# Query absorption and the first sample scores moved into the cached keys' expansion

## The reference, cut to what matters

```python
# streams: 512 cached latents each, 16 new tokens, 16 heads
kvb    = (c_kv @ w_kv_b).reshape(b, S, 16, 64 + 64)
k_nope = rmsnorm(kvb[..., :64], k_norm)      # needs 1/rms per key and head
v      = kvb[..., 64:]
s = (einsum('bqhd,bkhd->bhqk', q_nope, k_nope)
     + einsum('bqhr,bkr->bhqk', q_rope, k_rope)) * ATTN_SCALE
p = softmax(where(mask, s, -inf)); o = einsum('bhqk,bkhd->bqhd', p, v)
cq = rmsnorm(u @ w_dq, q_norm)               # q_norm: 512 factors
```

## Time and profile before

| | us |
|---|---|
| three runs | 1844.54, 1846.04, 1845.98; median 1845.98 |
| the profiled execution: its own time | 1845.79 |
| its span | 1844.0 |
| PE busy | 1814.8 (98%) |
| DVE busy | 1135.7 (62%) |
| ACT busy | 827.9 (45%) |
| expansion, y = 0 to 7 | about 1281 to 1394 in the span |
| absorption, first scores and units 0 to 15 | about 1395 to 1483 |

### The profile page before, as it was taken

One profiled execution on the slowest core, in us unless ns is written; L12 is line 12 of the kernel. 1 busy time (PEld: TensorE's weight loads), 2 busy tenths in 40 slices (PEclk: granted clock), 3 DMA queues, 4 the chain that ended last, 5 costly groups with the idle time before them and its releaser, 6 DMA issues.

```text
span 1844.0 us, 28274 instructions
## 1 busy us (share of the span) xinstructions
PE 1814.8 (98%) x10567; PEld 1739.3 (94%) x10567; DVE 1135.7 (62%) x1706; ACT 827.9 (45%) x1420; POOL 228.2 (12%) x278
## 2 busy tenths in 40 slices
PE   9999999999999999999999999999998999999998
PEld 9999999799888999999999999996777999999998
DVE  6454447879889745544775454456778856454445
ACT  5333335665564433333563333246665544333333
POOL 1000010311311000011400001122112131000110
PEclk9999999999999999999999999999999999999999
DMA  6434444456352544344343434451124534443442
GB/s 211 134 117 135 137 137 150 154 206 233 122 205 86 192 125 127 123 149 135 117 139 121 134 117 138 137 172 40 47 77 141 173 115 131 129 125 125 148 131 76
DMA packets 68388, 249.49 MB, mean 135 GB/s; under 512 B 8200, under 2 KB 10504, under 8 KB 67024
## 3 DMA queue, kind: packets, MB, share of 16 engines
q1 hardware_dynamic: 58880, 206.86, 36.6%
q0 software_dynamic: 9424, 41.48, 6.6%
HBM read 235.52 MB, written 12.12 MB: 134 GB/s over the span
## 4 chain that ended last, share of the span: by engine, by line
PE 88%; DVE 6%; ACT 3%; issue 1%; DMA 1%; POOL 0%; DVEq 0%; ACTq 0%; POOLq 0%
PE pair L1910 25%; PE pair L1912 25%; PE pair L1911 25%; PE pair L2419 2%; PE pair L2328 2%; PE pair L2330 2%; PE pair L2329 2%; DVE wlo L1242 1%; PE pair L2118 1%; PE pair L2276 0%; PE pair L2448 0%; PE pair L2135 0%; PE pair L1917 0%; PE pair L1919 0%; PE pair L1918 0%
## 5 line engine op out<-in xcount | busy, mean ns | idle before, releaser
L1910 PE MATMUL pair<-xh,whi 128*128 128x384 f32 x1960 | 660.8, 337 | 3.1 <-DVE xl L1252 2.3
L1912 PE MATMUL pair<-xh,wlo 128*128 128x384 f32 x1960 | 655.5, 334 | 0.0
L1911 PE MATMUL pair<-xl,whi 128*128 128x384 f32 x1960 | 655.4, 334 | 0.0
L1242 DVE TENSOR_TENSOR wlo<-raw,whi 128x1024 fp32r<-128x1024 f32 (+3 forms) x371 | 463.9, 1252 | 164.4 <-ACT whi L705 163.6
L705 ACT ACTIVATE whi<-raw 128x1024 fp32r<-128x1024 f32 (+2 forms) x369 | 378.3, 1029 | 266.0 <-PE pair L1912 261.7
L1910 PEld LDWEIGHTS pair<-xh,whi 128*128 128x128 f32 x1960 | 368.1, 188 | 9.9 <-issue 4.1
L1911 PEld LDWEIGHTS pair<-xl,whi 128*128 128x128 f32 x1960 | 368.1, 188 | 1.6 <-issue 1.0
L1912 PEld LDWEIGHTS pair<-xh,wlo 128*128 128x128 f32 x1960 | 368.1, 188 | 0.0
L1262 DVE TENSOR_TENSOR tg<-pair,rstd 128x384 f32<-128x384 f32 x88 | 49.0, 557 | 326.1 <-PE pair L1912 325.4
L1910 PE MATMUL pair<-ah,whi 128*128 128x384 f32 x704 | 238.0, 338 | 0.0
L1912 PE MATMUL pair<-ah,wlo 128*128 128x384 f32 x704 | 237.9, 338 | 0.0
(11 more groups left out here) (406 smaller groups left out, 2199.9 us busy)
## 6 DMA issues: line engine op xcount, KB each, us to landing
raw<-in_stream SPq DMA_DIRECT2D x372, 512.0 KB, 3.6
S<-in_ssm POOLq DMA_DIRECT2D x4, 2048.0 KB, 9.2
out_ssm_s<-S POOLq DMA_DIRECT2D x4, 2048.0 KB, 7.8
seg<-acs_rows POOLq DMA_DIRECT2D x12, 512.0 KB, 5.7
cTb<-in_cacheT POOLq DMA_DIRECT2D x10, 512.0 KB, 4.3
kn<-rs_rows SPq DMA_DIRECT2D x16, 264.0 KB
lowC<-in_cache SPq DMA_DIRECT2D x8, 512.0 KB, 3.2
lowA<-in_cacheT POOLq DMA_DIRECT2D x6, 512.0 KB, 5.3
```

What stands on the lines that cost most here:

```text
L1242: V.tensor_tensor(wlo[:, r, 0:w], raw[:, r, 0:w], whi[:, r, 0:w].bitcast(F32), ALU.subtract).then_inc(lo_ready, 1)
L1910: M(out, whi[:, r, ws], mh_(k), start=first and k == k0, stop=False)
L1911: M(out, whi[:, r, ws], ml_(k), start=False, stop=False)
L1912: ins = M(out, wlo[:, r, ws], mh_(k), start=False, stop=last and k == k1 - 1)
```

## The change

- `absorb(y-1)` is issued after the second item of y = 1 to 7, and `absorb(7)` after the third item of y = 7, with its ACT and DVE halves in the same places. The banks are now 3, 7, 3, 7, 3, 7, 3, 5. POOL loads the four quarters of `wkT` as the prompt's heads are done with that memory.
- In y = 7: `rope_split(0)`, both `keys_split` and `rope_split(1)`, `s_scores(0)`, `s_max(0)`, `s_exp(0)` and the normalisation of unit 0. Streams 0 and 1 get memory of their own for this (`early`), and the last stream's squares go to another place (`sqB`), so that SP may load the factors earlier.
- The factors are made in two halves of four streams. Streams 4 to 7 have their square root in unit 0 on ACT, followed by a reload of the exponential table, their reciprocals in unit 1 on DVE, and the transpose in unit 2 on PE.
- The 512 factors of the query norm move from `gains` to `gq`, at the end of the memory, with a DMA of their own at the start. Two unused columns of `gains` go.

```diff
@@ PE
+            def absorb(j):
+                pe.wait_ge(wkT_ld, 16 * (j // 2 + 1))
+                if j < MH // 2 - 1:
+                    pe.wait_ge(ol_ready, j + 1)
+                else:
+                    pe.wait_ge(p_masked, MH)
...
             for y in range(MH // 2):
+                last = y == MH // 2 - 1
...
                 for i in range(4):
                     past_expand(8 * y + i)
+                    if y and i == 1:
+                        absorb(y - 1)
+                    if last and i == 2:
+                        absorb(y)
+                if last:
+                    pe.wait_ge(past_rstd, 2)
+                    rs_turn(bank[4], 0, 4)
...
-                if y == MH // 2 - 1:
-                    pe.wait_ge(past_rstd, 3)
-                    rs_turn(bank[2], 0, 6)
+                if last:
+                    pe.wait_ge(qc_ev, 8)
+                    pe.wait_ge(rs_ev, 2)
+                    pe.wait_ge(stack_lo, 2)
+                    pe.wait_ge(filled, 5)
+                    s_scores(0)
                 past_expand(8 * y + 6)
                 past_expand(8 * y + 7)
...
-            for j in range(4):
-                absorb(j)
-            absorb(4)
-            absorb(5)
...
-            s_scores(0)
-            absorb(6)
-            absorb(7)
             for u in range(UNITS):
-                if u == 0:
-                    pe.wait_ge(qc_ev, 8)
                 if u + 1 < UNITS:
                     s_scores(u + 1)
-                if u == 1:
-                    pe.wait_ge(past_rstd, 4)
-                    rs_turn(bank[1], 6, 8)
+                if u == 0:
+                    pe.wait_ge(ol_ready, MH // 2)
+                    pe.wait_ge(past_sq, 8 * STREAMS)
                 if u == 3:
                     pe.wait_ge(rs_ev, 3)
                 if u >= 2:
                     s_values(u - 2)
+                if u == 2:
+                    pe.wait_ge(past_rstd, 4)
+                    rs_turn(bank[1], 4, 8)
@@ ACT
                 for i in range(3):
                     past_square(8 * y + i)
+                    if y and i == 1:
+                        absorb_hi(y - 1)
+                if last:
+                    absorb_hi(y)
+                    keys_split(0)
+                    act.wait_ge(rs_turn_ps, 2)
+                    A(rsT[0:4 * MH, :], bank[4][0:4 * MH, 0:3 * P], ACT.Copy)
+                    A(rsT2[0:4 * MH, 0:P], bank[4][0:4 * MH, 3 * P:4 * P], ACT.Copy).then_inc(rs_ev, 1)
                 p_turned(2 * y)
                 p_turned(2 * y + 1)
...
                 past_square(8 * y + 3)
-                if y + 1 < MH // 2:
+                if last:
+                    keys_split(1)
+                    rope_split(1)
+                else:
                     p_exp(2 * y + 2)
...
+                if last:
+                    act.preload_act_table(ACT.Exp)
                 past_square(8 * y + 6)
+                if last:
+                    s_exp(0)
+                if y == MH // 2 - 2:
+                    rope_split(0)
...
+                if u == 0:
+                    A(ksq[:, :, 4:8], ksq[:, :, 4:8], ACT.Sqrt, bias=EPS, scale=1.0 / NOPE).then_inc(past_std, 1)
+                    act.preload_act_table(ACT.Exp)
@@ DVE
                 for i in range(8):
+                    if not more and i == 7:
+                        s_norm(0)
                     past_sums(8 * y + i)
+                    if y and i == 1:
+                        absorbed(y - 1)
...
+                    if not more:
+                        if i == 0:
+                            rope_split(0)
+                        if i in (1, 2):
+                            if i == 2:
+                                absorbed(y)
+                            dve.wait_ge(past_std, 1)
+                            V.reciprocal(ksq[:, :, 2 * i - 2:2 * i], ksq[:, :, 2 * i - 2:2 * i]).then_inc(past_rstd, 1)
+                        if i == 2:
+                            keys_split(0)
+                        if i == 3:
+                            keys_split(1)
+                            rope_split(1)
+                        if i == 5:
+                            s_max(0)
...
+                if u == 1:
                     dve.wait_ge(past_std, 2)
-                    V.reciprocal(ksq[:, :, 6:8], ksq[:, :, 6:8]).then_inc(past_rstd, 1)
+                    for b in (4, 6):
+                        V.reciprocal(ksq[:, :, b:b + 2], ksq[:, :, b:b + 2]).then_inc(past_rstd, 1)
@@ SP and POOL
-            sp.wait_ge(past_sum, 8 * STREAMS)
+            sp.wait_ge(past_sum, 8 * (STREAMS - 1))
             rstd_rows(0)
...
-            for x in range(0, MH, MH // 4):
-                pool.wait_ge(qk_ps, x + MH // 4)
-                pool.dma_start(wkT[0:QD, x:x + MH // 4], T["wkT"][:, x:x + MH // 4]).then_inc(wkT_ld, 16)
+                if b % 2:
+                    x = MH // 4 * (b // 2)
+                    pool.wait_ge(qk_ps, x + MH // 4)
+                    pool.dma_start(wkT[0:QD, x:x + MH // 4], T["wkT"][:, x:x + MH // 4]).then_inc(wkT_ld, 16)
...
+            past_rope(0)
             past_keys(0)
-            past_rope(0)
+            past_rope(1)
+            past_keys(1)
             pool.wait_ge(rs_ev, 2)
```

More of the change, by code:

```diff
@@ L176, in build @@
             lowA = sb("lowA", [P, 4096], F32, mla)
-            lowB = sb("lowB", [P, 4096], F32, mla)
+            with ExitStack() as split:
+                lowB = sb("lowB", [P, 4096], F32, split)
+            early = sb("early", [P, 4096], F32R, mla)
             lowC = sb("lowC", [P, 2048], F32, mla)
@@ new lines, in s_max @@
+            def s_max(u):
+                s, o = u % 2, 64 + 8 * (u % 2)
+                p, r = (t[:, s, 0:KEYS].rearrange("p (a t) -> p a t", a=2) for t in (Pb, kn))
+                dve.wait_ge(pt_ps, MH + max(u - 1, 0))
+                dve.wait_ge(rk_ld[s], 16 * (u // 2 + 1))
+                dve.wait_ge(sc_ps, u + 1)
+                step(V.tensor_tensor(p, pair[1][:, :, 0:KEYS // 2], r, ALU.mult))
+                V.tensor_tensor(p, p, pair[2][:, :, 0:KEYS // 2], ALU.add).then_inc(s_added, 1)
+                dve.wait_ge(s_added, u + 1)
+                step(V.reduce_max(sm[:, o:o + 1], Pb[:, s, 0:KEYS], axis=AX.X))
+                V.tensor_scalar(sm[:, o + 2:o + 3], sm[:, o:o + 1], -SCALE, None, ALU.mult).then_inc(s_max_ready, 1)
@@ L1794, in _, with s_norm @@
+            def s_norm(u):
+                s, o = u % 2, 64 + 8 * (u % 2)
+                dve.wait_ge(s_exp_ready, u + 1)
+                step(V.reciprocal(sm[:, o + 5:o + 6], sm[:, o + 4:o + 5]))
+                V.tensor_scalar(Pb[:, s, 0:KEYS], Pb[:, s, 0:KEYS], sm[:, o + 5:o + 6], None, ALU.mult).then_inc(p_ready, 1)
             past_split(1)
@@ L2331, in past_expand, with s_scores @@
                 ins.then_inc(past_ps, 1)
+            def absorb(j):
+                pe.wait_ge(wkT_ld, 16 * (j // 2 + 1))
+                if j < MH // 2 - 1:
+                    pe.wait_ge(ol_ready, j + 1)
+                else:
+                    pe.wait_ge(p_masked, MH)
+                for k in range(2):
+                    for hh in range(2):
+                        x = 2 * j + hh
+                        ins = M(bank[QC_BANK[j]][:, tiles(2 * k + hh)], wkT[0:QD, x, tiles(k)], Qs[0:QD, :, x, :],
+                                start=True, stop=True)
+                ins.then_inc(qc_ps, 1)
+            def s_scores(u):
+                b, g = divmod(u, 2)
+                if g == 0:
+                    pe.wait_ge(past_lo, STREAMS + b + 1)
+                    pe.wait_ge(stack_lo, 2 + b + 1)
+                if u:
+                    pe.wait_ge(s_added, u)
+                for a in range(2):
+                    t, out = slice(264 * a, 264 * a + 264), pair[1][:, a, 0:264]
+                    for k in range(2):
+                        qh, ql = (q[:, k, b, 8 * g:8 * g + 8, :].rearrange("p h q -> p (h q)") for q in (QCh, QCl))
+                        M(out, qh, keys_hi(b)[:, k, t], start=k == 0, stop=False)
+                        M(out, qh, keys_lo(b)[:, k, t], start=False, stop=False)
+                        M(out, ql, keys_hi(b)[:, k, t], start=False, stop=k == 1)
+                for a in range(2):
+                    ins = M(pair[2][:, a, 0:264], q_stack(b)[0:3 * ROPE, g, :], k_stack(b)[:, 264 * a:264 * a + 264],
+                            start=True, stop=True)
+                ins.then_inc(sc_ps, 1)
             pe.wait_ge(q_kept, 12)
```

218 lines of the change are left out of this document (77 added, 141 removed).

## The result

The kernel after took 1848.99 us (1847.15 to 1850.89, 22 runs), the kernel before 1845.97 (1844.22 to 1847.79, 22 runs): ratio 1.0018, 95% interval 1.0012 to 1.0025. So it is slower by 3.0 us, a little within the 0.2% that the prediction called no change, and 2.0 us over its 1847.0. It looks like a small miss of a small effect. It is not: four terms of about 0.5 to 7 us add up to it, and the prediction had only the smallest at a price of its own. The profiled execution took 1850.78 us, its span 1849.0.

The account below looks back on a forecast made before the run. PE was taken as the bound, busy 1814.8 of 1844.0 us, with 6.25 us of seam waits to win. These go and some 7.5 come; with issue gaps +1.2 on 1845.8 gives 1847.0 us, range 1841.3 to 1850.0.

Parts of the forecast that it names:

- The absorptions lengthen the expansion by 5.6 us: Six absorptions move ahead of item 56, where PE is the bound: expansion 5.6 us longer, what follows shorter by the same.
- The four `wkT` loads are issued a y or more ahead of use ... cost 0, at worst one late quarter, a landing of 4.5 us: Loads on POOL during the expansion: costed at 0, at worst 4.5 us for one quarter landing late.
- The query norm's factors and the 64 bytes less of `gains` cost nothing that a row shows: Load at the start, hidden by 200 us of the first SwiGLU: cost nothing, or 2 us if not hidden.
- The last y and the factors: Layout of y = 7 from item 56: SP may load factors at 12.95 us, landing taken as 3.6, `s_max(0)` at 16.55.
- PE's wait for the turn: In y = 7 PE stands 1.3 us before turning the factors, waiting for DVE's two reciprocals.
- The layout's total: Absorptions 5.6 plus 41.2 us from item 56 to `s_values(2)`: 46.8 against 45.9 before; with issue gaps +1.2 us.
- From there PE is the bound in both kernels: From `s_values(2)`, 41.2 us after item 56, PE is busy 10.00 of 10.00 us, so no further difference.
- The table loads: Two ACT loads around unit 0's square root, 1.28 us each by the row; the skill's page would add 2.8 us.
- (a): Rival: the seam closes as ACT and DVE get through y = 7 faster; 1841.3 us, 1839.5 at most; chance 0.21.
- (b): Rival: seam partly closed, factors land early and ACT's unit 0 queue overlaps better; 2 us won, 1845; chance 0.20.
- (c): Rival: ACT's unit 0 queue longer, each table load holding twice its row; `s_values(0)` 2.6 us later, 1849.6; chance 0.10.
- (d): Rival: the factors land at the upper bound of 6.8 us, +3.2 us, 1850.2; chance 0.05.

Follow-up runs that it names:

- e1: Kernel before with only the query norm's factors moved to `gq` and `gains` 64 bytes per partition smaller: 1839.90 us, ratio 0.9967.
- e3: Kernel after with the second quarter of `wkT` issued before POOL waits to copy the stack: 1842.30 us, ratio 0.9981 to the kernel before.
- e4: e3 with SP's factor loads issued ahead of its value loads: 1840.35 us, ratio 0.9970 to the kernel before.
- e5: e4 with a second pair of ACT table loads in unit 0: 1843.29 us, ratio 0.9983 to the kernel before.
- e6: e4 with the square root and its table loads, the reciprocals and the turn two units later: 1842.33 us, ratio 0.9980 to the kernel before.
- e8: Kernel before's work with small tiles moved so that `ah` and `al` start at 64 modulo 256 bytes: 1839.53 us.
- e11: Kernel before's work with `gains` and `rows` moved to the end, so that `ah` and `al` start at 128 modulo 256 bytes: 1840.06 us.

## Why the prediction was right, and where it was wrong

The forecast of +1.2 us, no change, came near +3.0 by luck: mistakes of +8.7 and -6.1 us cancelled for the most part. The medians divide it so: address -6.1 (e1 less before), `wkT` +6.7 (after less e3), SP's order +2.0 (e3 less e4), the moved work +0.45 (e4 less e1); together +3.0.

**The absorptions lengthen the expansion by 5.6 us: right.** From the first prompt scores to item 56 are 105.8 us before, 110.8 in e4: +5.0, 0.83 for each of six, near the 0.93 of the earlier trace rows. Their halves on ACT and DVE cost nothing, as predicted: PE stays at 13.00 of 13.00 us from 1360.

**"The four `wkT` loads are issued a y or more ahead of use ... cost 0, at worst one late quarter, a landing of 4.5 us": wrong, +6.7.** This is the step that failed. The issue stands a y ahead in the code, but its queue doesn't: POOL waited 15.11 us for ACT to finish the stack, copied four times (2.3 us), and issued the quarter at 1322.96, 0.65 us before PE stood. The landing was 4.5 as the bad end had it, but the sum took 0. The prediction said that POOL "waits for the ends of the y there anyway" and didn't look at the copies between, though the diff has them; and even the bad end left out the lower clock behind the wait, 2.4 us.

**"The query norm's factors and the 64 bytes less of `gains` cost nothing that a row shows": wrong, -6.1.** No row of before could show it, yet its bound was given on one side only (2 us of loss), and no end was set to what a shift of all later tiles may do. The 2.7 ns that it was, over 2112 matmuls, are the second largest term.

**The last y and the factors: right.** In us from item 56:

| | predicted | after | e4 |
|---|---|---|---|
| PE's wait for the turn | 1.3 | 1.00 | 1.00 |
| SP issues the factors | 12.95 | 12.77 | 12.77 |
| `s_max(0)` starts | 16.55 | 17.06 | 16.99 |
| `s_scores(1)` starts | 18.5 | 18.56 | 18.49 |
| `s_values(0)` starts | 30.9 | 31.98 | 31.03 |
| `s_values(2)` starts | 41.2 | 43.06 | 41.93 |

The factors landed in 4.21 us, between the bounds 2.2 and 6.8, 0.6 later than the value taken. (The prediction's own terms for SP, 10.1 + 0.3 + 0.5 + 2.2, make 13.1 and not 12.95, and ACT's from 24.5 make 30.7 and not 30.85. Neither changes the total by more than 0.2.) Wait by wait it was rougher. e4, with the prediction's value in brackets: transposes of unit 0 0.74 (0.3), `s_scores(2)` 1.10 (1.6), transposes of unit 1 0.55 (0.75), `s_scores(3)` 1.56 (0.85), `s_values(0)` 1.18 (2.35), `s_values(1)` 0.93 (0.5). What `s_scores(3)` stood longer is the late load of unit 2's factors, which the prediction left out, and with PE that much later the wait for ACT is shorter. The layout's total in e4 is 5.0 + 41.93 = 46.9 against 45.9 before: +1.0 for a forecast of +1.2. In the kernel after it is 1.1 more, with a clock of 0.66 from 1410 to 1415 and a wait of 1.97 instead of 1.10 before `s_scores(2)`.

**"From there PE is the bound in both kernels": wrong in the kernel after, +2.0.** PE had 8.36 of 10.00 us from 1430. The prediction followed SP's queue only as far as the first factors; before, the same order of SP did no harm: it issued the factors of unit 6 at 1424.69, and DVE used them at 1431.66 without a wait. In the kernel after they went out at 1428.87, and DVE stood 2.46 us for them until 1437.36, PE 1.64 and 0.48. e4, where it is mended, has the 10.00.

**The table loads: right, by the row.** Each took 1.28 us with nothing beside it. The Trainium skill (ScalarE: Activation LUTs, "What ACT_TABLE_LOAD costs") adds about 1380 ns of drain to each load, by which the estimate was 1849.8 us. That is close to what was measured, which shows how little one total proves: e5 has twice the loads and is 2.5 to 2.9 us slower, near the two rows' 2.56 and not the 5.3 of that section, and its queue has no gap.

**The rivals.** (a) and (b), the seam closing: excluded, 7.1 us of waits in e4. (c), ACT's queue longer: the wait exists, but at its row's price. (d), the factors at their bound: 4.21, no; it was the third load of factors that landed late, beside the loads of values that (d) names. What made the time was none of the rivals: an address, a late quarter and SP's order.

## What to carry to other kernels

A load that is written early isn't issued early: walk its queue up to the issue and ask what each instruction ahead of it waits for, for every load of the moved step and once more for the queue at the place where time was won. Removing or adding a small tile moves everything behind it; here that alone was worth 6 us, so time such an edit by itself before reading anything into the rest. When a large reordering comes out near zero, split it before believing that it did nothing: here 6 us of gain hid 9 us of loss. When work moved off a late queue wins nothing, as in e6, follow the chain that ended last to where it is paid again.

## What the runs showed of the hardware

- Where a matmul's moving operand starts in a partition mattered: `ah` and `al` at 0 modulo 256 bytes gave 175.1 ns a matmul of 384 columns, at 64, 128 or 192 it was 172.4 to 172.8. Matmuls of the same shape on `xh` and `xl`, which didn't move, kept their rate (521 in 90 us before and after). Whether it is this operand or another tile moved with it isn't settled.
- A wait of 3.86 us on PE was followed by 4.9 us of matmuls at half the rate, 0.43 us against 0.23 (granted clock 0.77 over the 15 us). Waits of 1 to 2 us close together were followed by a fall in some executions (0.50 to 0.87 over 5 us) and not in others: behind the same wait of 2.10 us the clock was 0.66 in e1 and 1.00 in before, e8 and e11.
- Table loads on ACT take 1.28 us each, also three in a row, with 0.01 us between.
- A load of factors (264 KB) landed 4.1 to 4.3 us after its issue when it was the first, and 7.6 to 9.1 us after it when it was the third and two loads of 512 KB (8.1 us to landing) stood ahead of it on the same queue.
